# A product-key expert layer on one Trainium2 core: three of four token blocks go from gathered expert rows to a dense layer with a gate matrix

## The chip, the cores and the metric

One core of one Trainium2 chip runs the program. The metric is device time in microseconds of that core. The engines are TensorE (PE; its weight loads are listed as PEld), VectorE (DVE), ScalarE (ACT), GpSimd (POOL) and SyncE (SP), each with its own queue; they meet by semaphores. All data is float32.

## The reference

One decoder layer on x (1 x 512 x 1024):

```python
proj = x @ w_in                                   # 1024 -> 3584: seven groups of 512 columns
r = silu(rg) * GroupNorm(retention(rotary(rq), rotary(rk), rv))   # 4 heads of 128
d = 0.8 * RMSNorm((softmax(q1 k1^T) - lam * softmax(q2 k2^T)) v)  # 4 heads, causal
x = LayerNorm(alpha * x + concat(r, d) @ w_out)
q = (x @ w_query)                                 # 8 heads x 2 halves x 128
s = q . sub_keys                                  # 128 keys for each half
top_s, top_i = top_k(s, 16)                       # per half; then the best 16 of 256 sums
expert_idx = top_i[0] * 128 + top_i[1]            # 16384 experts
gate = softmax(best 16 sums)
ffn[t] = sum_e gate[t,e] * gelu(x[t] . u[expert_idx[t,e]]) * v[expert_idx[t,e]]   # 128 e per token
x = LayerNorm(alpha * x + ffn)
```

`peer_u` and `peer_v` are 16384 x 1024 each, 64 MB each. A token uses 128 of the 16384 rows of each.

## The kernel before

The 512 tokens are four blocks of 128. The work goes in two waves (`WAVES`, line 51): block 0 alone, then blocks 1 to 3. Each wave loads all 13 weight pieces of 2 MB (seven of `w_in`, two of `w_out`, four of `w_query`), so each is read twice.

**Mixer.** `fill_psum` (L509 and L515) runs the projections as eight accumulating matmuls per 512-wide bank. Rotary, decay, the norms, softmax's maxima and joins are on DVE; the exponentials and most copies out of PSUM are on ACT. `attend` (L661 scores, L681 transposes, L685 mix) goes head by head, then `mixed_out` transposes (L707) and multiplies by `w_out` (L716, L587 for block 0). `ln1` is LayerNorm 1. `query` (L744) makes the queries, 128 columns wide for block 0 and 384 for the second wave, and the key scores (L754).

**Retrieval.** `retrieve(b, s)` on DVE (L1269 to L1311) finds the 16 best keys and pairs of two heads of one block: `best_keys`, `best_pairs`, `best_experts`. A block has four such quarters, sixteen in all.

**Experts, block 0.** POOL gathers one row per token and expert slot (L438, 512 KB for 128 tokens, u rows and v rows separately) into a ring of 8. `dots` (L1039) multiplies a u row by the token and sums, on DVE. 32 v rows are added on PE through a diagonal matrix of gates (L461), 96 on DVE by `sums` (L1052). These groups of four, `rows(n)`, are interleaved by hand with the second wave's mixer work.

**Experts, blocks 1 to 3.** For each of 3 x 128 slots POOL gathers the u row and the v row of each token in one transfer of 1 MB (L426) into a ring of 18. DVE does the dot product (`pair_dot`, L1060), ACT the gelu of four slots (L971), DVE the weight (`weigh`, L1067), ACT writes the gates onto a diagonal (L979), PE adds v rows with two matmuls of 512 columns per slot (`add_pairs`, L474). The slot of the ring is free when PE has added it. The remaining ten quarters of the retrieval lie inside this loop on DVE. Last come `join_sums` and `finish` (LayerNorm 2) of each block.

## Time and profile before

| | |
|---|---|
| median of 3 runs | 1660.17 us (1654.67 to 1662.5) |
| span of the profiled execution, first to last instruction | 1633.5 us |
| PE busy | 1276.5 us (78%) |
| DVE busy | 1155.6 us (71%) |
| ACT busy | 267.2 us (16%) |
| POOL busy | 625.2 us (38%) |
| DMA moved | 603.44 MB, mean 369 GB/s |
| mean granted clock of PE | 0.896 |

The profiled execution's own time outside the profiler is not given apart from the three runs; its span lies 26.7 us under their median. Busy time is the union of an engine's instructions.
### The profile page before, as it was taken

What the parts mean: (1) busy time and instruction counts of PE and PEld (TensorE: products, weight loads), DVE (VectorE), ACT (ScalarE), POOL (GpSimd) and SP (SyncE); (2) the same over time, 40 slices, a digit from 0 to 9 for tenths busy, and PEclk for the clock granted to TensorE, in tenths of its full rate; (3) what the DMA queues carried; (4) which work ended last, traced back from release to release, by engine and by line L of the source; (5) the groups of instructions that cost most, each with busy time, mean ns of one, the idle gap of its engine ahead of it and who ended that gap; (6) DMA issues with size and microseconds to landing.
All of it is one profiled execution on the core that took longest, in us unless ns stands there. A gap on an engine that the chain in (4) does not pass through costs nothing.

```text
span 1633.5 us, 11511 instructions
## 1 busy us (share of the span) xinstructions
PE 1276.5 (78%) x3448; PEld 618.1 (38%) x3448; DVE 1155.6 (71%) x2727; ACT 267.2 (16%) x754; POOL 625.2 (38%) x645
## 2 busy tenths in 40 slices
PE   7879979888646994586978687878777878787885
PEld 5465446433323562232323233333333333332332
DVE  1349999767798979987676767776767677764454
ACT  0110000121211111121212121212121212121111
POOL 0004344474445565543434343434342434343320
PEclk9989999999767997798888888989897989899899
DMA  9939798897759898999999999999999999999993
GB/s 339 390 140 353 280 344 312 319 409 274 263 189 335 319 373 329 410 422 421 422 421 421 422 422 421 422 421 422 421 422 421 422 421 422 421 422 421 421 422 127
DMA packets 125710, 603.44 MB, mean 369 GB/s; under 512 B 12624, under 2 KB 14928, under 8 KB 76368
## 3 DMA queue, kind: packets, MB, share of 16 engines
q0 software_dynamic: 92160, 536.91, 81.2%
q1 hardware_dynamic: 33488, 65.80, 11.0%
q8 instruction: 27, 0.44, 0.1%
q14 instruction: 35, 0.29, 0.1%
HBM read 600.57 MB, written 2.10 MB: 369 GB/s over the span
## 4 chain that ended last, share of the span: by engine, by line
DMA 38%; PE 31%; DVE 23%; issue 3%; POOL 2%; SPq 1%; ACT 1%; DVEq 0%; POOLq 0%
DMA arena<-uv,idx 37%; PE W L474 7%; PE W L509 7%; DVE arena L1060 5%; PE ACC L474 4%; DVE xs L1052 4%; PE W L744 3%; PE W L716 3%; PE ACC L461 2%; POOL arena L438 2%; PE W L515 2%; DVE arena L1039 1%; DMA arena<-w_in 1%; DVE cand L1301 1%; DVE cand L1303 1%
## 5 line engine op out<-in xcount | busy, mean ns | idle before, releaser
L474 PE MATMUL W<-arena,fdiag 128*128 128x512 f32 x1024 | 498.9, 648 | 170.1 <-ACT fdiag L979 170.1
L426 POOL DMA_INDIRECT arena<-uv,idx x384 | 367.5, 957 | 586.7 <-PE W L474 355.7
L1060 DVE SCALAR_TENSOR_TENSOR arena<-arena,X 128x1024 f32<-128x1024 f32 x256 | 309.2, 1219 | 200.8 <-DMA arena<-uv,idx 199.7
L438 POOL DMA_INDIRECT arena<-uv,idx x256 | 257.3, 1005 | 372.2 <-DVE idx L1311 125.1
L474 PEld LDWEIGHTS W<-arena,fdiag 128*128 128x128 f32 x1024 | 208.6, 208 | 459.7 <-issue 253.0
L474 PE MATMUL ACC<-arena,fdiag 128*128 128x512 f32 x512 | 254.9, 660 | 69.3 <-ACT fdiag L979 69.3
L1060 DVE SCALAR_TENSOR_TENSOR arena<-arena,W 128x1024 f32<-128x1024 f32 x128 | 154.8, 1219 | 95.8 <-DMA arena<-uv,idx 95.4
L474 PEld LDWEIGHTS ACC<-arena,fdiag 128*128 128x128 f32 x512 | 107.0, 213 | 217.2 <-issue 132.1
L979 ACT ACTIVATE fdiag<-ident,gate 128x128 f32<-128x128 f32 x384 | 123.3, 390 | 354.7 <-DVE gate L1067 351.0
L1039 DVE SCALAR_TENSOR_TENSOR arena<-arena,X 128x1024 f32<-128x1024 f32 x128 | 150.0, 1216 | 24.8 <-DMA arena<-uv,idx 24.3
L509 PE MATMUL W<-arena 128*128 128x512 f32 x320 | 143.7, 605 | 9.7 <-DMA arena<-w_in 9.0
L1052 DVE SCALAR_TENSOR_TENSOR xs<-arena,gate,xs 128x1024 f32<-128x1024 f32 x96 | 123.3, 1284 | 19.3 <-DMA arena<-uv,idx 11.1
L744 PE MATMUL W<-arena 128*128 128x128 f32 (+1 forms) x512 | 116.8, 391 | 1.4 <-ACT arena L912 1.4
L971 ACT ACTIVATE hid<-hid 128x4 f32<-128x4 f32 x96 | 19.7, 205 | 456.5 <-DVE arena L1060 456.5
L744 PEld LDWEIGHTS W<-arena 128*128 128x128 f32 x512 | 80.2, 198 | 36.2 <-ACT arena L912 2.2
L509 PEld LDWEIGHTS W<-arena 128*128 128x128 f32 x320 | 60.8, 194 | 81.9 <-issue 76.9
L515 PE MATMUL W<-arena 128*128 128x128 f32 (+1 forms) x256 | 58.9, 388 | 10.8 <-DVE arena L1157 9.4
L461 PE MATMUL ACC<-arena,fdiag 128*128 128x512 f32 x128 | 59.0, 615 | 4.2 <-DMA arena<-uv,idx 4.2
L515 PEld LDWEIGHTS W<-arena 128*128 128x128 f32 x256 | 39.0, 194 | 28.4 <-issue 11.8
L716 PE MATMUL W<-arena 128*128 128x512 f32 x96 | 43.8, 616 | 0.7 <-ACT arena L912 0.7
L461 PEld LDWEIGHTS ACC<-arena,fdiag 128*128 128x128 f32 x128 | 24.5, 197 | 36.0 <-issue 29.7
L716 PEld LDWEIGHTS W<-arena 128*128 128x128 f32 x96 | 18.7, 198 | 25.1 <-issue 23.2
(178 smaller groups left out, 824.7 us busy)
## 6 DMA issues: line engine op xcount, KB each, us to landing
arena<-w_in SPq DMA_DIRECT2D x13, 2048.0 KB, 13.8
arena<-peer_w_query SPq DMA_DIRECT2D x8, 2048.0 KB, 14.4
arena<-uv,idx POOLq DMA_INDIRECT x640, 25.4
arena<-w_out SPq DMA_DIRECT2D x4, 2048.0 KB, 14.9
arena<-w_in SPq DMA_DIRECT2D x4, 512.0 KB, 6.4
out<-xs SPq DMA_DIRECT2D x4, 512.0 KB, 8.1
arena<-xT SPq DMA_DIRECT2D x1, 1536.0 KB, 18.2
xs<-x SPq DMA_DIRECT2D x1, 1536.0 KB, 17.0
```

The source lines that it names most:

```text
L426: pool.indirect_dma_start(out=fused[slot], out_offset=None, in_=uv, in_offset=bass.IndirectOffsetOnAxis(ap=idx[:, E + n:E + n + 1], axis=0 ...
L438: pool.indirect_dma_start(out=ring[:, r, :], out_offset=None, in_=rows, in_offset=bass.IndirectOffsetOnAxis(ap=idx[:, e:e + 1], axis=0), e ...
L461: last = nc.tensor.matmul(ACC[:, half * HW:(half + 1) * HW], fdiag[:, e % ND, :], ring[:, r, half * HW:(half + 1) * HW], start=e == 0, sto ...
L474: last = nc.tensor.matmul(sum_of(b)[:, half * HW:(half + 1) * HW], fdiag[:, n % ND, :], fused[n % NS][:, D + half * HW:D + (half + 1) * HW ...
L509: last = nc.tensor.matmul(bank, actT[:, k, part * P:(part + 1) * P], wts[slot][:, k, :], start=(k == 0), stop=(k == KD - 1))
L515: last = nc.tensor.matmul(bank[:, at:at + n_tok], wts[slot][:, k, h * P:(h + 1) * P], actT[:, k, toks], start=(k == 0), stop=(k == KD - 1))
L716: last = nc.tensor.matmul(W[:, 2 + half, :], mixT[:, k, :], wts[slot][:, k, :], start=(k == 0), stop=(k == KD - 1))
L744: last = nc.tensor.matmul(dst, wts[slot][:, k, i * P:(i + 1) * P], actT[:, k, toks], start=(k == 0), stop=(k == KD - 1))
L979: nc.scalar.activation(fdiag[:, n % ND, :], ident[:], ACT.Copy, scale=gate[:, E + n:E + n + 1]).then_inc(pair_diag_ready, 1)
L1039: STT(out=ring[:, r, :], in0=ring[:, r, :], scalar=1.0, in1=X[:], op0=ALU.mult, op1=ALU.mult, accum_out=hid[:, e:e + 1]).then_inc(slot_use ...
L1052: STT(out=xs[:, 0, :], in0=ring[:, r, :], scalar=gate[:, e:e + 1], in1=xs[:, 0, :], op0=ALU.mult, op1=ALU.add).then_inc(slot_used[r], 1)
L1060: STT(out=fused[slot][:, 0:D], in0=fused[slot][:, 0:D], scalar=1.0, in1=token_of(b), op0=ALU.mult, op1=ALU.mult, accum_out=hid[:, E + n:E ...
```

## The change

The mixer runs once for all four blocks: 28 projection banks in one go, then `attend` and `mixed_out` for blocks 0 to 3, and block 0's queries and key scores are placed beside blocks 1 and 2's attention (`beside`). Each weight piece of the mixer is read once, `w_query` twice. Block 0 still gathers its rows, 256 transfers of 512 KB into a ring of 6; DVE does all dots and all sums.

Blocks 1 to 3 gather nothing. Their expert layer is computed for all 16384 experts, in 128 tiles of 128 experts: `up` multiplies a tile of u (from a transposed copy `uT` that the host lays out) by 384 tokens, `hidden` applies gelu, `mask_hidden` multiplies by the gate matrix, which is zero for experts that the token did not pick, `add` multiplies by the tile of v for each of three blocks. The gate matrix is built token by token: DVE writes two one-hot matrices (`hot_quads`: picks x first key, and picks x second key), PE multiplies them (`quad`, four tokens at a time, each 128 x 128 columns), ACT copies the result to a staging tile and sends 2 MB of it per 32 tokens to a DRAM tensor `gd` of 25 MB (`take_quad`); it is read back by `load_g`, four tiles of experts at a time. 47 tiles of the hidden layer are held (`NH`): 23 are made before the gate matrix, 24 during it, and 81 in the last loop.

The order of the work is written out by hand in each engine's block. The core of the diff (lines that only rename or drop the old loops are left out):

```diff
+W_SLOTS = [0, 1, 2, 3, 0, 1, 2] + [0, 1] + [3, 2, 3, 2] + [0, 1, 0, 1]
+Q0, Q1 = WIN + WOUT, WIN + WOUT + WQ
+ROWS = 2 * E
+RING = 6
+ND = NB - 1
+TD = ND * P
+NT = P
+NH = 47
+UR = 4
+VR = 4
+LEAD = 6
+TAIL = 4
+QUADS = P // 4
+OH_RING = 4
+OH_BANKS = 5
+CHUNK = 32
+NC = TD // CHUNK
+PER_CHUNK = CHUNK // 4
+GT = 4
+UP_FIRST = NH - ND * QUADS // 4
...
+            def load_u(n):
+                if n >= UR:
+                    sp.wait_ge(u_ready, n - UR + 1)
+                elif n < 2:
+                    sp.wait_ge(diff_mixed, NB)
+                else:
+                    sp.wait_ge(mixer_ready, 2 * NB)
+                sp.dma_start(u_ring[n % UR], uT[n].rearrange("p (k e) -> p k e", k=KD)).then_inc(u_landed[n % UR], 16)
+            def load_v(n):
+                if n >= VR:
+                    sp.wait_ge(v_done, n - VR + 1)
+                sp.dma_start(v_ring[n % VR], uv[n * P:(n + 1) * P, D:2 * D]).then_inc(v_landed[n % VR], 16)
+            def load_g(g):
+                if g >= 2:
+                    sp.wait_ge(masked, GT * (g - 1))
+                src = gd[:, :, g * GT:(g + 1) * GT, :].rearrange("c j i t -> j c (i t)")
+                sp.dma_start(g_ring[g % 2], src).then_inc(g_landed[g % 2], 16)
...
+            for i in range(5, Q1 + 2):
+                load_w(i)
+            for n in range(UR):
+                load_u(n)
+            for i in range(Q1 + 2, Q1 + WQ):
+                load_w(i)
+            for n in range(UR, NH + UR):
+                load_u(n)
+            for i in range(2):
+                sp.wait_ge(spill_landed[i], 16 * (NC // 2))
+            load_g(0)
+            for n in range(VR):
+                load_v(n)
+            load_g(1)
+            sp.wait_ge(quad_ready, ND * QUADS)
+            for n in range(NT):
+                if n + VR < NT:
+                    load_v(n + VR)
+                if n + NH + UR < NT:
+                    load_u(n + NH + UR)
+                if n % GT == 1 and n // GT + 2 < NT // GT:
+                    load_g(n // GT + 2)
...
+            for s in range(ROWS):
+                e = s % E
+                if s < E and e % QUARTER == 0:
+                    pool.wait_ge(experts_ready, e // QUARTER + 1)
+                if s >= RING:
+                    pool.wait_ge(row_used[s % RING], s // RING)
...
+            def beside(b, h):
+                if (b, h) == (1, 1):
+                    turn_x1(0)
+                elif (b, h) == (1, 2):
+                    query_0(0)
+                elif (b, h) == (1, 3):
+                    query_0(1)
+                    key_scores_0(0)
+                elif (b, h) == (2, 0):
+                    query_0(2)
+                    key_scores_0(1)
+                elif (b, h) == (2, 1):
+                    query_0(3)
+                    key_scores_0(2)
+                elif (b, h) == (2, 2):
+                    key_scores_0(3)
+                elif (b, h) == (2, 3):
+                    turn_x1(1)
+                elif (b, h) == (3, 1):
+                    turn_x1(2)
...
+            def up(n):
+                pe.wait_ge(u_landed[n % UR], 16 * (n // UR + 1))
+                if n >= 2:
+                    pe.wait_ge(h_ready, n - 1)
+                for k in range(KD):
+                    last = nc.tensor.matmul(X[:, n % 2, 0:TD], u_ring[n % UR][:, k, :], actT[:, k, P:S],
+                                            start=(k == 0), stop=(k == KD - 1))
+                last.then_inc(u_ready, 1)
+            def turn_picks(d):
+                pe.wait_ge(pk_ready, d + 1)
+                if d:
+                    pe.wait_ge(pT_ready, d)
+                for c in range(3):
+                    last = nc.tensor.transpose(ACC[:, 1, c * P:(c + 1) * P], pk[d % 2][:, c, :], ident[:])
+                last.then_inc(pk_turned, 1)
+            def quad(q):
+                pe.wait_ge(hot_ready, q + 1)
+                if q >= OH_BANKS:
+                    pe.wait_ge(quad_taken, q - OH_BANKS + 1)
+                bank = quad_bank(q)
+                for m in range(4):
+                    last = nc.tensor.matmul(bank[:, m * P:(m + 1) * P], b_hot[:, q % OH_RING, m, :],
+                                            a_hot[:, q % OH_RING, m, :], start=True, stop=True)
+                last.then_inc(quad_ready, 1)
+            def add(n, d):
+                for half in range(2):
+                    last = nc.tensor.matmul(sum_banks(d)[:, half, :], h_slot(n)[:, d * P:(d + 1) * P],
+                                            v_ring[n % VR][:, half * HW:(half + 1) * HW],
+                                            start=(n == 0), stop=(n == NT - 1))
+                return last
...
+            project()
+            score(0, 0)
+            for b in range(NB):
+                attend(b)
+                mixed_out(b)
+            turn_x1(NB - 1)
+            query()
+            pe.wait_ge(scores_stored, 4 + ND * WQ)
+            for n in range(UP_FIRST):
+                up(n)
+            for d in range(ND):
+                turn_picks(d)
+                for q in range(d * QUADS, (d + 1) * QUADS):
+                    quad(q)
+                    if q % 4 == 3:
+                        up(UP_FIRST + q // 4)
+            pe.wait_ge(quad_taken, ND * QUADS)
+            for n in range(NT - TAIL):
+                pe.wait_ge(masked, n + 1)
+                pe.wait_ge(v_landed[n % VR], 16 * (n // VR + 1))
+                for d in range(ND):
+                    last = add(n, d)
+                last.then_inc(v_done, 1)
+                if n + NH < NT:
+                    up(n + NH)
+            pe.wait_ge(masked, NT)
+            for i in range(VR):
+                pe.wait_ge(v_landed[i], 16 * (NT // VR))
+            for d in range(ND):
+                for n in range(NT - TAIL, NT):
+                    last = add(n, d)
+                last.then_inc(acc_ready, 1)
...
+            def hidden(n):
+                act.wait_ge(u_ready, n + 1)
+                if n >= NH:
+                    act.wait_ge(v_done, n - NH + 1)
+                elif n >= 42:
+                    act.wait_ge(experts_ready, 16)
+                elif n >= 37:
+                    act.wait_ge(experts_ready, 12)
+                elif n >= 32:
+                    act.wait_ge(experts_ready, 8)
+                elif n >= 26:
+                    act.wait_ge(experts_ready, 4)
+                nc.scalar.activation(h_slot(n), X[:, n % 2, 0:TD], ACT.Gelu).then_inc(h_ready, 1)
+            def take_picks(d):
+                act.wait_ge(experts_ready, 4 * d + 8)
+                nc.scalar.activation(pk[d % 2][:, 2, :], pk[d % 2][:, 2, :], ACT.Exp).then_inc(pk_exp_ready, 1)
+                act.wait_ge(pk_turned, d + 1)
+                if d == 2:
+                    act.wait_ge(hot_ready, QUADS)
+                nc.scalar.activation(pT[d % 2], ACC[:, 1, 0:3 * P].rearrange("p (c t) -> p c t", c=3),
+                                     ACT.Copy).then_inc(pT_ready, 1)
+            def take_quad(q):
+                c, at = divmod(q, PER_CHUNK)
+                act.wait_ge(quad_ready, q + 1)
+                if at == 0 and c >= 2:
+                    act.wait_ge(spill_landed[c % 2], 16 * (c // 2))
+                nc.scalar.activation(stage[c % 2][:, :, 4 * at:4 * at + 4],
+                                     quad_bank(q).rearrange("p (m i) -> p i m", m=4), ACT.Copy).then_inc(quad_taken, 1)
+                if at == PER_CHUNK - 1:
+                    act.wait_ge(quad_taken, q + 1)
+                    nc.scalar.dma_start(gd[c], stage[c % 2]).then_inc(spill_landed[c % 2], 16)
...
+            project()
+            for b in range(NB):
+                attention(b)
+                take_mixed(b)
+            take_x1(NB - 1)
+            query()
+            act.wait_ge(experts_ready, 4)
+            nc.scalar.activation(gate[:], gate[:], ACT.Exp).then_inc(gate_exp_ready, 1)
+            for n in range(UP_FIRST):
+                hidden(n)
+            for d in range(ND):
+                take_picks(d)
+                for q in range(d * QUADS, (d + 1) * QUADS):
+                    take_quad(q)
+                    if q % 4 == 3:
+                        hidden(UP_FIRST + q // 4)
+            for n in range(NH, NT):
+                hidden(n)
+                if n == NH + 60:
+                    for i in range(RING):
+                        last_dot = max(s for s in range(E) if s % RING == i)
+                        act.wait_ge(row_used[i], last_dot // RING + 1)
+                    nc.scalar.activation(hid[:], hid[:], ACT.Gelu).then_inc(gelu_ready, 1)
...
+            def dot(s):
+                r = s % RING
+                dve.wait_ge(row_landed[r], row_landings(s))
+                STT(out=ring[r], in0=ring[r], scalar=1.0, in1=xs[:, 0, :], op0=ALU.mult, op1=ALU.mult,
+                    accum_out=hid[:, s:s + 1]).then_inc(row_used[r], 1)
+            def weigh():
+                gate_norm(gate[:], gate_exp_ready, 1)
+                residual(0)
+                dve.wait_ge(gelu_ready, 1)
+                link(TT(out=gate[:], in0=gate[:], in1=hid[:], op=ALU.mult))
+            def add_row(s):
+                r = s % RING
+                dve.wait_ge(row_landed[r], row_landings(s))
+                if s > E:
+                    dve.wait_ge(row_used[(s - 1) % RING], (s - 1) // RING + 1)
+                STT(out=xs[:, 0, :], in0=ring[r], scalar=gate[:, s - E:s - E + 1], in1=xs[:, 0, :],
+                    op0=ALU.mult, op1=ALU.add).then_inc(row_used[r], 1)
...
+            def norm_picks(d):
+                dve.wait_ge(pk_exp_ready, d + 1)
+                g = pk[d % 2][:, 2, :].rearrange("p (h k) -> p h k", h=PH)
+                link(nc.vector.reduce_sum(gsum[:], g, AX.X))
+                link(nc.vector.reciprocal(gsum[:], gsum[:]))
+                TT(out=g, in0=g, in1=gsum[:].unsqueeze(2).to_broadcast([P, PH, TOPK]),
+                   op=ALU.mult).then_inc(pk_ready, 1)
+            def hot_quads(d):
+                dve.wait_ge(pT_ready, d + 1)
+                for q in range(d * QUADS, (d + 1) * QUADS):
+                    if q >= OH_RING:
+                        dve.wait_ge(quad_ready, q - OH_RING + 1)
+                    for m in range(4):
+                        t = 4 * (q % QUADS) + m
+                        TS(b_hot[:, q % OH_RING, m, :], iota_f[:], pT[d % 2][:, 1, t:t + 1], None, ALU.is_equal)
+                        last = TS(a_hot[:, q % OH_RING, m, :], iota_f[:], pT[d % 2][:, 0, t:t + 1],
+                                  pT[d % 2][:, 2, t:t + 1], ALU.is_equal, ALU.mult)
+                    last.then_inc(hot_ready, 1)
+            def mask_hidden(n):
+                g = n // GT
+                if n % GT == 0:
+                    dve.wait_ge(g_landed[g % 2], 16 * (g // 2 + 1))
+                dve.wait_ge(h_ready, n + 1)
+                h = h_slot(n).rearrange("p (c t) -> p c t", c=NC)
+                TT(out=h, in0=h, in1=g_ring[g % 2][:, :, n % GT * CHUNK:(n % GT + 1) * CHUNK],
+                   op=ALU.mult).then_inc(masked, 1)
...
+                    if (b, h) in ((2, 1), (3, 1)):
+                        best_keys(0, b - 2)
+                    elif (b, h) in ((2, 2), (3, 2)):
+                        best_pairs()
+                    elif (b, h) in ((2, 3), (3, 3)):
+                        best_experts(0, b - 2)
...
+            best_keys(0, 2)
+            best_pairs()
...
+            best_experts(0, 2)
+            retrieve(0, 3)
+            rows(8)
+            for s in range(4):
+                retrieve(1, s)
+            best_keys(2, 0)
+            norm_picks(0)
+            best_pairs()
+            best_experts(2, 0)
+            hot_quads(0)
+            for s in range(1, 4):
+                retrieve(2, s)
+            best_keys(3, 0)
+            norm_picks(1)
+            best_pairs()
+            best_experts(3, 0)
+            hot_quads(1)
+            for s in range(1, 4):
+                retrieve(3, s)
+            norm_picks(2)
+            rows(4)
+            hot_quads(2)
+            for n in range(LEAD):
+                mask_hidden(n)
+            for n in range(NT):
+                if n + LEAD < NT:
+                    mask_hidden(n + LEAD)
+                if n == 62:
+                    weigh()
+                rows(min(2, E - taken[0]) if n < 62 else 2)
+                if n == NT - 1:
+                    rows(ROWS - taken[0])
+                    finish(0)
+            for d in range(ND):
+                join_sums(d)
+                finish(d + 1)
```

## Rows read from the trace of the kernel before

**Rows 1.** Stretches: PE, PEld, DVE, ACT, POOL busy; PEclk, DMA share, GB/s

```profile
150.00:200.00 50.00, 50.00 (x136) 23.44 (x135) 48.76 (x133) 4.67 (x8) 18.20 (x20) 1.00 0.82 314
...
450.00:500.00 50.00, 21.02 (x73) 12.20 (x72) 45.78 (x83) 9.44 (x26) 22.47 (x19) 0.60 0.61 208
...
800.00:1000.00 200.00, 158.49 (x320) 66.96 (x320) 134.37 (x344) 39.27 (x111) 74.93 (x80) 0.88 1.01 421
```

**Rows 2.** Chain that ended last, shares, from the page

```profile
DMA 38%; PE 31%; DVE 23%; issue 3%; POOL 2%; SPq 1%; ACT 1%; DVEq 0%; POOLq 0%
DMA arena<-uv,idx 37%; PE W L474 7%; PE W L509 7%; DVE arena L1060 5%; PE ACC L474 4%; DVE xs L1052 4%; PE W L744 3%; PE W L716 3%; PE ACC L461 2%; POOL arena L438 2%; PE W L515 2%; DVE arena L1039 1%; DMA arena<-w_in 1%; DVE cand L1301 1%; DVE cand L1303 1%
```

**Rows 3.** Who waited for whom

```profile
ACT fdiag L979 <- DVE gate L1067: 351.0, 95, 7.4
DVE arena L1060 <- DMA arena<-uv,idx: 295.2, 246, 2.2
```

**Rows 4.** Groups by line and form: us busy, mean ns

```profile
L474 PE MATMUL W<-arena,fdiag 128*128 128x512 f32 x1024 | 498.9, 648 | 170.1 <-ACT fdiag L979 170.1
...
L1060 DVE SCALAR_TENSOR_TENSOR arena<-arena,X 128x1024 f32<-128x1024 f32 x256 | 309.2, 1219 | 200.8 <-DMA arena<-uv,idx 199.7
...
L474 PE MATMUL ACC<-arena,fdiag 128*128 128x512 f32 x512 | 254.9, 660 | 69.3 <-ACT fdiag L979 69.3
...
L1052 DVE SCALAR_TENSOR_TENSOR xs<-arena,gate,xs 128x1024 f32<-128x1024 f32 x96 | 123.3, 1284 | 19.3 <-DMA arena<-uv,idx 11.1
```

**Rows 5.** Pieces of the chain in order of time: start, length

```profile
108.46 7.16 PE W L744 x64
...
187.09 20.62 PE W L509 x48
...
259.25 5.16 PE W L515 x16
```

**Rows 6.** PE in order of time: first projection, attention, output, queries

```profile
6.03 8.62 PE L509 MATMUL W<-arena 128*128 128x512 f32 x16 [6.03 <-DMA arena<-w_in]
...
428.09 1.65 PE L685 MATMUL W<-arena 128*128 128x128 f32 x6 [0.58 <-ACT arena L888]
434.93 1.97 PE L707 MATMUL W<-ident,arena 128*128 128x128 f32 x8 [5.19 <-DVE arena L1243]
...
439.89 14.00 PE L716 MATMUL W<-arena 128*128 128x512 f32 x32
...
466.82 2.08 PE L661 MATMUL W<-dkT,arena 64*128 64x512 f32 x4 [9.06 <-ACT arena L880]
...
476.34 2.08 PE L661 MATMUL W<-dkT,arena 64*128 64x512 f32 x4
...
503.73 15.82 PE L716 MATMUL W<-arena 128*128 128x512 f32 x32 [0.69 <-ACT arena L912]
...
530.04 23.22 PE L744 MATMUL W<-arena 128*128 128x384 f32 x64 [0.69 <-ACT arena L912]
...
626.52 3.00 PE L754 MATMUL W<-arena 128*128 128x128 f32 x24 [0.58 <-ACT arena L929]
...
1615.56 7.13 PE L474 MATMUL W<-arena,fdiag 128*128 128x512 f32 x16 [0.62 <-ACT fdiag L979]
```

**Rows 7.** DVE in order of time: first and last of a retrieval quarter

```profile
555.67 0.87 DVE L1269 MAX8 best_v<-rv 128x8 f32<-128x128 f32 x4 [0.76 <-ACT rv L935]
...
571.26 0.19 DVE L1311 SCALAR_TENSOR_TENSOR idx<-sel 128x32 int32<-128x32 f32 x1
```

**Rows 8.** DVE groups by form, small scalar operations

```profile
L1189 DVE TENSOR_SCALAR arena<-W,mv,rstd 128x128 f32<-128x128 f32 x16 | 5.5, 404 | 0.1
...
L1214 DVE TENSOR_SCALAR arena<-arena,rz 128x256 f32<-128x256 f32 x4 | 1.5, 372 | 0.1
```

**Rows 9.** DMA issues by source: count, KB each, median us to landing

```profile
arena<-w_in SPq DMA_DIRECT2D x13, 2048.0 KB, 13.8
...
arena<-xT SPq DMA_DIRECT2D x1, 512.0 KB, 3.8
```

More of the change, by code:

```diff
@@ L806, in take_fill @@
                     act.wait_ge(proj_ready, n + 1)
[L807 to L814 removed]
+                    act.wait_ge(rot_ready, rots(n))
@@ L873, in attention, with project @@
-            def attention(b, beside):
+                    dst = {RV: rv, DV: dv, DQ: dqT, DKK: dkT}[g][:, part, :]
+                    nc.scalar.activation(dst, bank, ACT.Copy).then_inc(proj_taken_act, 1)
+                if n and FILLS[n - 1][0] in (RQ, RK):
+                    take_rotated(rots(n) - 1)
+            def project():
+                for n in range(len(FILLS)):
+                    take_fill(n)
+                    if n == fills_of(RV)[0]:
+                        act.wait_ge(lam_dots_ready, 1)
+                        nc.scalar.activation(lam[:, 2:4], lam[:, 0:2], ACT.Exp).then_inc(lam_exp_ready, 1)
@@ L874, in attention @@
+            def attention(b):
                 keys_n = (b + 1) * P
@@ new lines, in store_scores, with query @@
+            def store_scores(b, s, bank):
+                act.wait_ge(keys_scored, 4 + ND * s + b if b else s + 1)
+                nc.scalar.activation(scores[b][:, s * HW:(s + 1) * HW], bank, ACT.Copy).then_inc(scores_stored, 1)
+            def query():
+                for n in range(4, 20):
+                    s, i = divmod(n - 4, 4)
+                    act.wait_ge(query_ready, n + 1)
+                    if s and i == 0:
+                        act.wait_ge(keys_scored, 4 + s * ND)
+                    nc.scalar.activation(qq[:, i, :], W[:, 2 + n % 2, 0:TD], ACT.Copy).then_inc(query_taken, 1)
+                    if i == 3:
+                        for j in range(ND):
+                            store_scores(1 + j, s, W[:, (s * ND + j) % 2, :])
```

998 lines of the change are left out of this document (304 added, 694 removed).

## The prediction

> **What bounds the kernel now.** I read the chain first, then the waits, then the stretches. The chain [rows 2] gives 37% of the span to the gathers of experts (uv by idx) and 31% to PE in many small shares: no engine's own work sets most of the end, the transfers do. The stretches [rows 1] show where. From 650 us on, memory moves 421 or 422 GB/s without a pause: 384 slots of 1 MB, about 403 MB, in some 970 us. PE is busy for only 158.48 of 200 us there, with a granted clock of 0.88, and both waits [rows 3] agree: DVE waited 295.2 us for gathered rows, and ACT waited 351.0 us for the weights that DVE makes from them. Before 650 us it is another kernel: PE has stretches with no gap at all (50.00 of 50 us at clock 1.00) and stretches with long ones (21.02 of 50 at 0.60), where attention goes head by head.
>
> So the question is whether 403 MB of gathers at 422 GB/s cost more than what stands in for them. The new work is PE's, so I need PE's price at full clock. A projection bank, eight matmuls of 512 columns, takes 20.62 / 3 = 6.87 us [rows 5], so 0.859 us per matmul; eight of 384 columns take 5.16 us, 0.645 each; 32 of 128 columns take 7.16 us, 0.224 each. `up` has the same form as the 384-column row, `add` and `fill_psum` that of the 512-column one.
>
> **PE's work alone.** up: 128 tiles x 5.16 = 660 us. add: 128 x 6 x 0.859 = 660 us. The gate matrix: 384 x 0.224 = 86 us. Projections: 28 x 6.87 = 192 us. Output: 4 x 14.0 = 56 us [rows 6]. Queries: 4 x 7.16 + 16 x 5.16 = 111 us. Key scores, retention and transposes: some 50 us. Sum about 1815 us, without a single wait, against a span of 1633.5 us. What goes: 768 add matmuls of the same form, which took 498.9 + 254.9 = 754 us of busy time at the lower clock [rows 4] and were hidden by the gathers. What the change saves in DMA (some 360 MB left of 603: 134 for both tables, 134 of gathers, 50 for the gate matrix, the rest weights) was the bound, but PE's sum is already longer than the whole kernel.
>
> **The new order, stage by stage.**
>
> Projections. PE starts at 6.0 us [rows 6]; 28 banks are 192.4 us; four transposes for each of 8 rotated banks cost 0.5 us (half of 1.97 us for eight, which ran at half clock), so 4; retention's 80 matmuls of 128 columns are 18 us. The rest of xT is in the queue ahead of the second bank, a few us: 4. End at 224 us. The weights don't hold it: a 2 MB piece lands in 13.8 us [rows 9] and lasts 27.5.
>
> Attention and output, four blocks. A head of block 3 took 476.34 - 466.82 = 9.5 us with four gathered rows on DVE in it [rows 6]; they cost 4 x 1.28 [rows 4], which leaves 4.4 us. Sixteen heads: 70. From the last mix of a block (429.7) to its output matmuls (439.9) are 10.2 us of squares, norm, transposes and copies: 41. Output 56. LN1 delays the second head of three blocks by about 5: 15. What stands `beside`: 4 x 7.16 + 4 x 1.9 + 3 x 2.0 = 42 on PE, of which each of 11 pieces hides about 1 behind the join: 31. DVE's six thirds of two retrieval quarters (15.8 us each, 555.67 to 571.45 [rows 7]) are 32, a third of it beside PE's pieces: 21. The first head of three blocks runs under the output matmuls: -12. Sum 222, and 10.5 from the last output matmul to the first query (519.55 to 530.04): 456 us.
>
> Queries. The code of the second wave is unchanged, 530.04 to 629.52 is 99.5 us: 556 us. Block 1's retrieval on DVE, four quarters of 15.8, keeps pace and ends by 575.
>
> First 23 ups: 119 us, to 675. Here the change adds a wait: `take_picks(0)` stands behind `hidden(22)` in ACT's queue, so the exponentials that `norm_picks(0)` needs come only now, and DVE, queued behind that wait with block 2's and 3's retrieval, idles for some 95 us. Then best_pairs and best_experts (two thirds of 15.8) and the transposes: 12, to 687.
>
> Gate matrix. Four quads and an up are 16 x 0.224 + 5.16 = 8.7 us of PE; a block is 8 of these, with waits 73 us. DVE has to write 32 one-hot tiles in the same time. No row has this form. Above stands the 128-column operation with two scalars from PSUM, 5.5 / 16 = 0.344 us [rows 8]; below, the four 128-wide operations in 0.87 us, 0.22 each [rows 7]; a 256-column one with one scalar from SBUF, 0.372, lies outside but shows that the second scalar and PSUM are what makes 0.344. I take 0.25, so 8.0 us: hidden by 8.7, barely. At 0.344 it is 11.0 and DVE sets the pace. Three blocks: 219. Between blocks PE has nothing: three quarters of retrieval, best_keys, then pairs and experts, 64 us less the 7 that DVE is ahead, so 57; and before the third, three quarters, the exponentials and four rows, 54 - 7 = 47. That gives 687 + 219 + 104 = 1010.
>
> Spill and read back. The last 2 MB go out (13.8 us as a load [rows 9], my only price) and 768 KB in runs of 512 bytes come back (3.8 us for 512 KB in such runs, so 5.8): 20. At 422 GB/s both would take 7, at 13.8 each 28; these are the bounds. To 1030.
>
> Last loop. 768 adds are 660, 81 ups 418: 1078 us, to 2108. What lies under it: DVE per tile one 384-wide product (about 0.55, from 1219 ns for 1024 columns [rows 4]) and two rows (2.6) against 10.3 and later 5.15; the DMA moves 2.3 MB in 10.3 us, later 1.8 MB in 5.15, 344 GB/s against 422 shown. `load_g` waits for `masked` and holds the loads of u and v queued on SP behind it, but DVE is six tiles ahead. Cost taken: 0. At the 314 GB/s of the stretch from 150 us [rows 1] the last 47 tiles would take 0.5 us more each, 23 us; if each of their 12 gate loads stalls PE for its own landing, 60; that is the upper bound. No gain below 0, since PE's matmuls are all there.
>
> End. From PE's last four matmul pairs (1622.7) to the span's end, 10.8 us [rows 6]: 2119. The profiled span lies 26.7 us under the median of the runs, so the time is 2119 + 27 = 2146 us.
>
> **A rule against the rows.** The rows give 0.859 us for a 512-column float32 matmul in an unbroken stream, as three banks back to back in 20.62 us show [rows 5]. The Trainium skill, TensorE: Matmul & The Clock Gate, section Back-to-back issue gap, gives a sustained spacing of about 131 ns for 512 columns in a stream of weight loads and matmuls, and 216 ns for an isolated one; its page FP8 and Floating Point Precision counts four passes for true float32. Four of the first are an estimate of 524 ns, four of the second 864 ns. The trace sides with the second. By the first the sum would be about 515 us shorter, 1631 us.
>
> **Rivals.**
> *The stream gets cheaper* (the other side: faster). Place: `up` and `add`. If a stream a thousand us long overlaps its passes better than one of 50 us, the 1320 us of the two shrink; the point is 486 us, that is 0.54 us per 512 columns in place of 0.859. At 0.53 the kernel takes 1640 us. Against it: stretches of 20.62 us and 50.00 of 50 us busy show no trend. The Trainium skill's 131 ns, above, is this rival. Chance 0.03, a third of it within half a per cent of no change.
> *DVE sets the pace of the gate matrix.* 0.344 per one-hot tile: 88 us per block in place of 73, and the 7 us ahead are lost: +60, 2206 us. For it: only 0.7 us lie between the two engines. Chance 0.19.
> *The clock.* If small waits in the last loop keep the granted clock at 0.88, as in the gathering stage [rows 1], 1078 becomes 1225: 2293 us. Against it: it was 1.00 wherever PE had no gap. Chance 0.09.
> *The front is shorter.* If the pieces beside attention hide in its gaps (52 us) and the retrieval overlaps somewhat better: -60, 2086 us. Chance 0.19.
> My forecast, 2146 us with its own range of 2110 to 2190, has 0.50.
>
> **How the numbers follow.** Half a per cent of 1660 us is 8 us, about what a measurement of this kernel can tell from no change. Every case but the first lies over 400 us above it, so slower gets 0.97, faster 0.02, the same 0.01. The range takes in the shorter front (2086, and 26 below for the spill and the ends of the heads), the gate matrix at DVE's pace and nearly all of the clock's case: 2060 to 2290.
>
> **What would show it.** In the new profile: PE busy near 1800 us and over 85%; 128-tile loop of about 10.3 us per tile down to 5.15, with clock 1.00; DVE idle about 95 us before the first picks are normed and PE idle twice for about 50 us in the gate stage; one-hot operations near 0.25 us; DMA around 360 MB. Wrong: `up` at under 5 us per tile, or a last loop that starts before 900 us.

## The result

The changed kernel takes 2126.62 us, median of 4 runs (2124.38 to 2129.2), against 1658.34 us for the kernel before, run beside it: a ratio of 1.282, 95% interval 1.279 to 1.284. The forecast was 2146, between 2060 and 2290.

The page of the profiled execution (span 2125.4 us, time 2127.21): the busy share of PE, the transfers, the chain that ended last, the costliest groups (busy, mean ns, idle before), and two DMA sources (count, KB, us to landing).

```profile
PE 1892.4 (89%) x6017; PEld 1042.1 (49%) x6017; DVE 957.2 (45%) x2767; ACT 207.8 (10%) x433; POOL 332.5 (16%) x261
...
DMA packets 149312, 366.78 MB, mean 173 GB/s; under 512 B 11120, under 2 KB 62576, under 8 KB 147568
...
PE 83%; DVE 12%; DMA 2%; ACT 1%; issue 1%; POOL 0%; SPq 0%; DVEq 0%
PE X L663 30%; PE W L690 19%; PE ACC L690 10%; PE W L460 6%; PE W L644 4%; PE W L591 3%; PE W L683 3%; PE W L457 3%; PE ACC L619 1%; DMA arena<-gd 1%; PE ACC L683 1%; DVE lng L1193 1%; DVE cand L1161 1%; DVE cand L1159 1%; PE W L653 1%
...
L663 PE MATMUL X<-arena 128*128 128x384 f32 x2048 | 678.0, 486 | 0.7 <-ACT dkT L838 0.7
...
L690 PE MATMUL W<-arena 128*128 128x512 f32 x768 | 349.6, 598 | 16.7 <-DMA arena<-uv 16.7
L1204 DVE TENSOR_TENSOR arena<-arena 128x384 f32<-128x384 f32 x96 | 52.6, 555 | 487.2 <-DMA arena<-gd 487.2
...
L690 PE MATMUL ACC<-arena 128*128 128x512 f32 x384 | 180.3, 592 | 0.0
...
L1193 DVE TENSOR_SCALAR lng<-iota_f,both_uses 128x128 f32<-128x128 f32 x384 | 137.2, 357 | 0.0
...
L1192 DVE TENSOR_SCALAR arena<-iota_f,both_uses 128x128 f32<-128x128 f32 x384 | 114.0, 297 | 21.5 <-PE W L683 16.8
...
L683 PE MATMUL W<-lng,arena 128*128 128x128 f32 x616 | 81.3, 290 | 23.3 <-DVE lng L1193 23.3
...
gd<-arena ACTq DMA_DIRECT2D x12, 2048.0 KB, 6.5
arena<-gd SPq DMA_DIRECT2D x32, 768.0 KB, 6.1
```

The chain has turned over [rows 2]: 83% PE where the gathers had 38%. PE is busy for 1892.4 us, more than the whole kernel before. `up` (L663) is 678.0 us, and `add` (L690) 349.6 + 180.3 = 529.9 in the records shown (1152 of its 1536 records are in these groups; the rest lie in groups by other home tiles of the hidden layer). The records of `up` are its 1024 matmuls, two for each. PE's busy time is 77 us over the 1815 us of my sum, which counted every matmul at full clock; the stretch of attention below ran at 0.76. What else makes up the 77 us was not taken apart. The bytes fell from 603.44 to 366.78 MB, and the time did not follow them.

The stretches, with the columns of [rows 1]:

```profile
224.00:456.00 232.00, 155.16 (x659) 96.86 (x660) 124.54 (x426) 41.97 (x135) 5.79 (x6) 0.76 0.18 62
456.00:557.00 101.00, 98.00 (x355) 61.08 (x354) 74.38 (x271) 15.28 (x29) 10.59 (x8) 0.97 0.27 99
557.00:677.00 120.00, 119.31 (x374) 70.31 (x373) 19.40 (x90) 13.25 (x26) 0.00 (x0) 1.00 0.31 97
677.00:778.00 101.00, 73.95 (x388) 56.03 (x387) 89.74 (x381) 28.19 (x46) 0.00 (x0) 0.88 0.35 131
778.00:822.00 44.00, 1.92 (x8) 1.52 (x8) 42.14 (x164) 0.80 (x2) 0.00 (x0) 0.50 0.00 0
...
1062.00:1500.00 438.00, 438.00 (x1191) 226.10 (x1190) 112.28 (x202) 21.12 (x43) 109.15 (x83) 1.00 0.65 222
...
1895.00:2110.00 215.00, 207.76 (x481) 91.45 (x479) 133.91 (x158) 0.00 (x0) 95.40 (x74) 0.98 0.84 306
```

In the last loop PE is busy 438.00 of 438 us at clock 1.00 and the DMA moves 222 GB/s; in the gathering stage [rows 1] PE had 79% at 0.88 and the DMA 421. The stretch of 778 to 822 is the opposite, PE 1.92 of 44 us while DVE works 42.14.

PE in order of time (start, length; in brackets the idle time before and who ended it). First three pieces round the first ups, then the gaps between the blocks of the gate matrix with the start of the last loop, then PE's last matmuls:

```profile
558.35 118.95 PE L663 MATMUL X<-arena 128*128 128x384 f32 x368 [0.69 <-ACT dkT L838]
680.45 0.55 PE L673 MATMUL ACC<-ident,both_uses 128*128 128x128 f32 x3 [3.15 <-DVE both_uses L1181]
692.53 6.81 PE L683 MATMUL W<-lng,arena 128*128 128x128 f32 x32 [11.53 <-DVE lng L1193]
```

```profile
808.90 0.90 PE L673 MATMUL ACC<-ident,both_uses 128*128 128x128 f32 x3 [43.26 <-DVE both_uses L1181]
820.98 3.89 PE L683 MATMUL W<-lng,arena 128*128 128x128 f32 x16 [11.18 <-DVE lng L1193]
...
932.37 0.90 PE L673 MATMUL ACC<-ident,both_uses 128*128 128x128 f32 x3 [38.51 <-DVE both_uses L1181]
938.77 2.08 PE L683 MATMUL ACC<-lng,arena 128*128 128x128 f32 x8 [5.50 <-DVE lng L1193]
...
1006.36 5.33 PE L663 MATMUL X<-arena 128*128 128x384 f32 x16
1021.18 6.13 PE L690 MATMUL W<-arena 128*128 128x512 f32 x8 [9.50 <-DMA arena<-uv]
```

```profile
2106.62 3.60 PE L690 MATMUL ACC<-arena,rv 128*128 128x512 f32 x8
```

The first 23 ups run 118.95 us without a break. Between the first and the second block's quads PE waits 43.26 + 11.18 us, between the second and third 38.51 + 5.50, and before the last loop 9.50. Waits of other engines, and PE's own by line (us, times, longest):

```profile
POOL arena L421 <- DVE arena L939: 1033.6, 17, 442.6
...
DVE arena L1204 <- DMA arena<-gd: 487.2, 24, 39.2
...
DVE gsum L1179 <- ACT both_uses L870: 102.8, 2, 102.4
```

```profile
PE ACC L673 <- DVE both_uses L1181: 84.9, 3, 43.3
PE W L683 <- DVE lng L1193: 23.3, 3, 11.5
...
PE W L690 <- DMA arena<-uv: 16.7, 2, 9.5
```

DVE's 102.4 us on `gsum` are the wait for the exponentials, which stand behind the first 23 `hidden` in ACT's queue. DVE waits 487.2 us more for the gate matrix in the last loop, which costs nothing, since it is ahead of PE there; PE itself waits for data 16.7 us in all.

### The profile page after: what moved, and what is told of

It reads as the page before. It is cut to its first block, busy times and chain, and to the rows that moved or that the text cites. A ratio compares the mean times of both kernels' runs of the same rounds, so it can differ in the third digit from the quotient of the medians.

```text
span 2125.4 us, 16625 instructions
## 1 busy us (share of the span) xinstructions
PE 1892.4 (89%) x6017; PEld 1042.1 (49%) x6017; DVE 957.2 (45%) x2767; ACT 207.8 (10%) x433; POOL 332.5 (16%) x261
## 2 busy tenths in 40 slices
DMA packets 149312, 366.78 MB, mean 173 GB/s; under 512 B 11120, under 2 KB 62576, under 8 KB 147568
## 4 chain that ended last, share of the span: by engine, by line
PE 83%; DVE 12%; DMA 2%; ACT 1%; issue 1%; POOL 0%; SPq 0%; DVEq 0%
PE X L663 30%; PE W L690 19%; PE ACC L690 10%; PE W L460 6%; PE W L644 4%; PE W L591 3%; PE W L683 3%; PE W L457 3%; PE ACC L619 1%; DMA arena<-gd 1%; PE ACC L683 1%; DVE lng L1193 1%; DVE cand L1161 1%; DVE cand L1159 1%; PE W L653 1%
## 5 line engine op out<-in xcount | busy, mean ns | idle before, releaser
L663 PE MATMUL X<-arena 128*128 128x384 f32 x2048 | 678.0, 486 | 0.7 <-ACT dkT L838 0.7
L421 POOL DMA_INDIRECT arena<-uv,idx x256 | 332.1, 1297 | 1752.0 <-DVE arena L939 1033.6
L663 PEld LDWEIGHTS X<-arena 128*128 128x128 f32 x2048 | 387.2, 190 | 282.9 <-issue 38.7
L690 PE MATMUL W<-arena 128*128 128x512 f32 x768 | 349.6, 598 | 16.7 <-DMA arena<-uv 16.7
L1204 DVE TENSOR_TENSOR arena<-arena 128x384 f32<-128x384 f32 x96 | 52.6, 555 | 487.2 <-DMA arena<-gd 487.2
L690 PEld LDWEIGHTS W<-arena 128*128 128x128 f32 x768 | 147.3, 192 | 190.0 <-issue 173.3
L690 PE MATMUL ACC<-arena 128*128 128x512 f32 x384 | 180.3, 592 | 0.0
L939 DVE SCALAR_TENSOR_TENSOR arena<-arena,xs 128x1024 f32<-128x1024 f32 x128 | 152.2, 1222 | 6.0 <-DMA arena<-uv,idx 5.6
L460 PE MATMUL W<-arena 128*128 128x512 f32 x320 | 142.9, 603 | 6.6 <-DMA arena<-w_in 6.3
L1193 DVE TENSOR_SCALAR lng<-iota_f,both_uses 128x128 f32<-128x128 f32 x384 | 137.2, 357 | 0.0
L1192 DVE TENSOR_SCALAR arena<-iota_f,both_uses 128x128 f32<-128x128 f32 x384 | 114.0, 297 | 21.5 <-PE W L683 16.8
L690 PEld LDWEIGHTS ACC<-arena 128*128 128x128 f32 x384 | 73.0, 190 | 91.8 <-issue 91.8
L683 PE MATMUL W<-lng,arena 128*128 128x128 f32 x616 | 81.3, 290 | 23.3 <-DVE lng L1193 23.3
L644 PE MATMUL W<-arena 128*128 128x384 f32 x256 | 85.7, 497 | 0.7 <-ACT arena L823 0.7
L591 PE MATMUL W<-arena 128*128 128x512 f32 x128 | 63.8, 662 | 0.7 <-ACT arena L815 0.7
L457 PE MATMUL W<-arena 128*128 128x512 f32 x128 | 56.1, 592 | 0.0
```

The lines of the kernel that those rows point to most:

```text
L421: pool.indirect_dma_start(out=ring[s % RING], out_offset=None, in_=rows, in_offset=bass.IndirectOffsetOnAxis(ap=idx[:, e:e + 1], axis=0), ...
L457: last = nc.tensor.matmul(bank, wts[slot][:, k, part * P:(part + 1) * P], actT[:, k, :], start=(k == 0), stop=(k == KD - 1))
L460: last = nc.tensor.matmul(bank, actT[:, k, part * P:(part + 1) * P], wts[slot][:, k, :], start=(k == 0), stop=(k == KD - 1))
L591: last = nc.tensor.matmul(W[:, 2 + half, :], mixT[:, k, :], wts[slot][:, k, :], start=(k == 0), stop=(k == KD - 1))
L644: last = nc.tensor.matmul(W[:, 2 + n % 2, 0:TD], wts[slot][:, k, i * P:(i + 1) * P], actT[:, k, P:S], start=(k == 0), stop=(k == KD - 1))
L663: last = nc.tensor.matmul(X[:, n % 2, 0:TD], u_ring[n % UR][:, k, :], actT[:, k, P:S], start=(k == 0), stop=(k == KD - 1))
```

## Experiments

The kernel before was run beside each group of runs, and the groups ran on different chips. Its time was 1658.34 us (median) beside the changed kernel, 1636.36 (median) beside e1 to e4, 1654.87 (median) beside e5 to e7, and 1648.39 (one run) beside e8 and e9. The times of e1, e5 and e6 are medians of four runs, those of e2, e3, e4, e7, e8 and e9 single runs. Savings are counted from the 2126.62 us of the changed kernel.

### The same work in a better order (e1)

```diff
 # ACT
+            for n in range(UP_FIRST):
+                hidden(n)
+                if n in (5, 18):
+                    exp_picks(n // 18)
 # PE and ACT: ups after which quad
-                    if q % 4 == 3:
-                        up(UP_FIRST + q // 4)
+UPS_AFTER = {4 * i + 3: (UP_FIRST + i,) for i in range(8)}
+UPS_AFTER[2 * QUADS - 1] = tuple(range(UP_FIRST + 8, UP_FIRST + 19))
+UPS_AFTER.update({2 * QUADS + 4 * i + 3: (UP_FIRST + 19 + i,) for i in range(5)})
+                    for n in UPS_AFTER.get(q, ()):
+                        up(n)
...
 # DVE, the new order
+            norm_picks(0)
+            for s in range(4):
+                retrieve(2, s)
+            norm_picks(1)
+            best_keys(3, 0)
+            best_pairs()
+            hot_quads(0)
+            hot_quads(1)
+            best_experts(3, 0)
+            for s in range(1, 4):
+                retrieve(3, s)
```

> Same work as the changed kernel, another order. ACT makes the exponentials of block 1's picks after hidden(5) and of block 2's after hidden(18) instead of behind hidden(22); DVE runs block 2's whole retrieval while PE does the first 23 ups; eleven of the ups that stood between quads stand together where DVE retrieves block 3. Theory (PE's own work sets the end, and the waits for DVE between the blocks of the gate matrix are added to it): the first quads start about 11 us earlier, PE's idle time of 43 + 11 us before the second block goes nearly away, of the 38 + 5 before the third too, and the quads without ups go at DVE's pace of about 7.2 us per four; last loop begins near 940 us in place of 1021, time 2050, ratio to before 1.235. Rival (the last loop is bound by something else that follows the clock on the wall, such as the row gathers of block 0): the loop grows by what the gate stage gives, time within 20 us of 2127.

Measured: 2062.29 us, ratio 1.260 (1.256 to 1.263), 64 us less than the changed kernel. PE in order of time, only pieces after a wait:

```profile
681.45 1.16 PE L686 MATMUL W<-lng,arena 128*128 128x128 f32 x8 [2.64 <-DVE lng L1203]
...
758.44 1.16 PE L686 MATMUL W<-lng,arena 128*128 128x128 f32 x8 [2.57 <-DVE lng L1203]
...
875.52 0.55 PE L676 MATMUL ACC<-ident,both_uses 128*128 128x128 f32 x3 [3.08 <-DVE both_uses L1191]
881.92 2.08 PE L686 MATMUL ACC<-lng,arena 128*128 128x128 f32 x8 [5.85 <-DVE lng L1203]
...
959.27 5.27 PE L693 MATMUL W<-arena 128*128 128x512 f32 x8 [13.95 <-DMA arena<-uv]
```

The quads start at 681.45 as expected, the second block's after 2.57 us of waiting, the third's after 3.08 + 5.85. The last loop starts at 959.27, 61.9 us earlier, and from there to the end of the span are 1102.3 us against 1104.2 in the changed kernel. So nearly all of the gain is idle time of PE, and none was given back. It was 12 us less than expected: quads without ups go at 1.81 us each, 57 us for a block, as forecast, but the third block, with five ups in it, took 63 us, and the wait for the gate matrix's way through DRAM grew to 13.95 us, for here no up follows the last quads and covers a part of it.

### Half of the adds, in both kernels (e2, e3)

```diff
 # add (changed kernel) and add_pairs (kernel before)
-                for half in range(2):
+                for half in range(1):
```

> The changed kernel; add makes only the first 512 of the 1024 output columns, so half of the v product of blocks 1 to 3 is left out. All transfers, all of DVE's and ACT's work stay. Theory (PE bound): 384 matmuls of 0.859 us go, 330 us, until the transfers or DVE take over; a tile costs 7.7 us in the first 81 and in the last 47, at 2.6 us of PE, the DMA's 1.8 MB at 400 to 422 GB/s set 4.3 to 4.5 us. So -209 - 35 = about -245 us: 1880. Rival (transfers set the last loop already): under 60 us less.

> The kernel before with the same edit: add_pairs makes only the first 512 of the 1024 output columns, half of the v product of blocks 1 to 3 is left out. All gathers stay. Theory (the gathers set the end, PE's 754 us are hidden): within 8 us of the kernel before, 1658. Rival (PE shares the bound): 50 us less or more.

Measured: 1888.71 us for the dense kernel, 238 less. The gathering kernel took 1633.58, where seven runs without the edit took 1633.61 to 1640.78: nothing that can be told from no change. Stretches of the dense one, then of the gathering one:

```profile
1021.00:1500.00 479.00, 479.00 (x1360) 258.61 (x1359) 165.59 (x296) 30.15 (x62) 156.78 (x116) 1.00 0.82 291
...
1648.00:1852.00 204.00, 137.58 (x284) 57.34 (x282) 127.99 (x127) 0.49 (x1) 98.16 (x82) 0.83 0.99 363
```

```profile
800.00:1000.00 200.00, 99.23 (x160) 38.74 (x159) 133.40 (x342) 38.84 (x110) 74.00 (x80) 0.75 1.01 421
```

One edit takes 384 matmuls out of either kernel, 330 us at full clock. In the gathering kernel PE falls from 158.49 to 99.23 busy us of 200 [rows 1], and even its granted clock falls, from 0.88 to 0.75; the transfers stay at 421 GB/s, as does the time. In the dense kernel PE stays at 479.00 of 479 and simply gets through sooner, until the last 47 tiles. They take 204 us, 4.3 each as expected; there PE is busy for 137.58 us, the DMA's share is 0.99, and the transfers have taken over. That is the bound changing hands, seen from both sides.

### Half of each up (e8)

```diff
-                for k in range(KD):
+                for k in range(KD // 2):
```

> The changed kernel; up contracts over only 512 of the 1024 features, four matmuls in place of eight, so half of each hidden value's sum is left out. Transfers stay. Theory (PE's sum sets the end wherever it is not waiting for DVE): the first 23 ups lose 59 us; the gate stage goes at DVE's 7.2 us in place of 8.7 per four quads, 24 groups, 35 us, but its gaps grow by the 7 us that DVE was ahead, twice, so 21; the 81 ups of the last loop lose 209. Together -289: 1838. Rival (the last loop falls to its transfers at 2.3 MB per 7.7 us, 300 GB/s): 60 us or more above that.

Measured: 1833.99 us, 293 less, where 289 were expected. In the last loop PE has no gap with 290 GB/s under it:

```profile
1000.00:1500.00 500.00, 500.00 (x1295) 245.69 (x1294) 176.18 (x292) 31.62 (x65) 162.41 (x125) 1.00 0.83 290
```

### Without block 0's rows (e4)

```diff
-            for s in range(ROWS):
+            for s in range(12):
                 e = s % E
...
 # DVE, last loop
-                rows(min(2, E - taken[0]) if n < 62 else 2)
```

> The changed kernel with block 0's experts left out except for the first 12 row gathers: 244 of 256 gathers, their dots and sums on DVE are gone. Theory (hidden under PE in the last loop): no change up to 8 us less, 2120 to 2127; what may go is a wait for v of some us at the loop's end. Rival (the gathers press on the transfers of u, v and the gate matrix or on DVE in the last 47 tiles): 20 to 60 us less.

The lines not shown let the wait for the rows, the gelu and the gates go over 12 columns, and drop the last `rows`. Measured: 2122.28 us, 4.3 less in a single run, and 2.1 under the fastest run of the changed kernel. The loop's stretch has half the traffic and the same PE:

```profile
1062.00:1500.00 438.00, 438.00 (x1191) 226.03 (x1190) 19.65 (x40) 21.07 (x43) 0.00 (x0) 1.00 0.37 120
```

244 gathers, 128 MB and 294 us of DVE's busy time (957.2 to 663.4) were hidden, but for these 4 us, of which 2.5 are PE's waits for tiles of v (16.7 to 14.2). The forecast's last loop took them as zero.

### The dense layer with cheap matmuls (e5, e6)

```diff
...
+        ub = part(16 * K, D).bitcast(BF).rearrange("p (i k e) -> p i k e", i=2, k=KD)
+        vb = part(16 * K + D, D).bitcast(BF).rearrange("p (i d) -> p i d", i=2)
+        xb = actT[:, :, 0:TD // 2].bitcast(BF)
 # ACT, one tile ahead of hidden(n)
+                    nc.scalar.activation(ub[:, n % 2], u_ring[n % UR], ACT.Copy).then_inc(u_cast, 1)
+                nc.scalar.activation(vb[:, n % 2], v_ring[n % VR], ACT.Copy).then_inc(v_cast, 1)
 # PE
-                    last = nc.tensor.matmul(X[:, n % 2, 0:TD], u_ring[n % UR][:, k, :], actT[:, k, P:S],
+                    last = nc.tensor.matmul(X[:, n % 2, 0:TD], ub[:, n % 2, k, :], xb[:, k, :],
 # DVE writes the masked hidden layer in bfloat16
-                TT(out=h, in0=h, in1=g_ring[g % 2]
+                TT(out=h_low(n).rearrange("p (c t) -> p c t", c=NC), in0=h, in1=g_ring[g % 2]
```

Not shown: the row ring's four slots in place of six, the new semaphores, the loads of u and v, which now wait for the cast and not for the matmul, and the last four tiles, whose adds go tile by tile in place of block by block.

> The changed kernel with up and add in bfloat16: ACT rounds each tile of u and v and the 384 tokens to bfloat16, the masked hidden layer is written in bfloat16, so the experts of blocks 1 to 3 are computed in lower precision; the row ring has 4 slots in place of 6 to make room. Bytes moved are the same. Theory (what made the dense layer slow is PE's price of 0.859 us for a float32 matmul of 512 columns): up and add fall to about a quarter, 1.3 us for each group of eight or six; the first 23 ups take about 42 us at ACT's pace, the gate stage goes at DVE's pace of 7.2 us per four quads, and the last loop is set by its transfers, 2.3 MB per tile at 422 GB/s or 5.5 us, later 4.3: 650 us in place of 1089. Time 1580, faster than the gathers. Rival (the mixed transfers, with 512-byte runs, don't pass 250 GB/s, or ACT's casts set the pace): last loop 850 us or more, time over 1780.

> The same in the order of e1: exponentials of the picks early, block 2's retrieval under the first ups, eleven ups together. Theory: DVE alone paces the gate stage now, and its idle time before the picks of block 1, some 25 us with the short ups, goes: 25 to 35 us less than e5, about 1550. Rival (the order gained by PE's idle time only, so with PE cheap it gives nothing): within 8 us of e5.

Measured: e5 1632.13 us, ratio 0.987 (0.984 to 0.990); e6, with e1's order, 1617.58 us, ratio 0.977 (0.974 to 0.980), beside 1654.87 for the kernel before. So 494 us of the changed kernel's 2126 went with the cheaper matmuls, although the same edit gives ACT two casts per tile and leaves the rows a smaller ring, and 15 more went with the order. These two kernels do lower-precision work against a kernel that stays in float32; the gathering kernel with bfloat16 tables was not tried. The last loop of e6 in its two parts, the 81 tiles with an up and the 47 without, then two waits of the second part:

```profile
901.00:1349.00 448.00, 262.75 (x1134) 113.35 (x1134) 220.76 (x349) 198.85 (x244) 164.12 (x147) 0.85 1.04 393
1349.00:1569.00 220.00, 102.33 (x282) 30.38 (x282) 131.69 (x132) 49.03 (x48) 98.88 (x87) 0.68 0.97 353
```

```profile
PE W L706 <- DVE arena L1254: 85.2, 32, 6.7
DVE xs L1005 <- DMA arena<-uv,idx: 81.0, 63, 4.3
```

In the first part the DMA's share is full, 393 GB/s, PE is busy for 262.75 of 448 us, and a tile takes 448 / 81 = 5.5 us, as expected. In the second 47 tiles were expected at 4.3 us, 202 us, and took 220 at 353 GB/s. There DVE waits for rows (81.0 us), its masking stands in the queue behind them, and PE waits for that (85.2 us). When PE has made its last add, at 1569 us, DVE still adds rows of block 0, to 1586, and then normalises four blocks one after another: 50 us to the end of the span, where the changed kernel needs 15.2. In e5 the two parts and the end are 443, 223.5 and 48 us, so of the 52 us by which it was over its expectation 17 are in the loop, expected at 650, and 33 behind it. Whether the ring of four rows did it was not tried by itself. e2, with six slots and no casts, moved the same last 47 tiles in 204 us and then took 35 to the end, which speaks for the ring or the casts, but doesn't part them. The order gave 15 us where 25 to 35 were expected. Three PE pieces of one tile:

```profile
1114.56 1.02 PE L706 MATMUL W<-arena,kT 128*128 128x512 bf16 x4 [1.01 <-ACT arena L883]
...
1115.42 0.59 PE L706 MATMUL ACC<-arena,kT 128*128 128x512 bf16 x2
...
1117.03 1.47 PE L679 MATMUL X<-arena 128*128 128x384 bf16 x8 [1.02 <-ACT arena L876]
```

The first four matmuls of 512 columns start at 1114.56 and the next at 1115.42, so they are 0.215 us apart, a quarter of float32's 0.859. Eight of 384 columns are listed with 1.47 us, the tail of the last one included, where float32's are listed with 5.33.

### The same without the rows (e9)

The edit of e4 on the kernel of e6.

> The kernel of e6 (bfloat16 up and add, the better order) with block 0's experts left out except for the first 12 row gathers. Theory (with PE's price gone the transfers set the last loop, 392 GB/s in e6): a tile moves 1.25 MB in place of 2.3, the loop goes at 3.2 to 3.6 us per tile and later at 1.8 to 2.7 in place of 5.9 and 4.8, so 300 us less than e6, 1320. The same edit took 5 us off the changed kernel, whose loop PE sets. Rival (the chain cast, up, gelu, mask sets e6's loop): under 100 us less.

Measured: 1284.36 us, 333 less than e6, where the same edit took 4 us off the changed kernel. The stretch lies in the tiles with an up:

```profile
900.00:1100.00 200.00, 173.29 (x868) 85.43 (x868) 30.54 (x63) 147.38 (x184) 0.00 (x0) 0.95 1.06 384
```

The transfers still run at 384 GB/s, with ACT's casts and PE close behind (147.38 and 173.29 of 200 us). A tile with an up takes 3.2 us, as expected, in place of e6's 5.5 (the expectation had e6's tiles at 5.9 and 4.8; its trace has 5.5 and 4.7). At nearly the same rate a tile moves 1.25 MB in place of 2.3, so there it is the bytes that cost. In the last 47 tiles and behind them the edit takes away transfers and DVE's work on rows together, and what each of the two costs was not separated. So the rows, which cost next to nothing under float32 matmuls, are worth a fifth of the kernel with cheap ones.

### The changed kernel again (e7)

> The changed kernel once more, on the chip of this call, where the kernel before may take 1636 us as in the last call or 1658 as in the first. Theory (before is set by the gathers' rate, which differs from chip to chip, the changed kernel by PE): 2127 within 4 us whichever the kernel before takes. Rival (the chips differ in everything alike): 2100 where the kernel before takes 1636.

Measured: 2128.03 us beside 1654.87. The kernel before was near its first value here, so this run doesn't tell the two theories apart. What speaks for the first is e1, beside which the kernel before took 1636.36: from the start of the last loop to the end of the span are 1102.3 us in e1, 1104.2 in the changed kernel and 1106.0 in this run. PE's loop is the same to 0.3% where the gathering kernel differs by 1.3%. A run of the changed kernel itself beside 1636 us was not made, and why the gathering kernel differs was not shown.

## Why the prediction was right

By its own steps, forecast and then measured:

| step | forecast | measured |
|---|---|---|
| first query on PE | 456 | 458.1 |
| queries | 99.5 | 100.2 (to 558.35) |
| first 23 ups | 119 | 118.95 |
| to the first quad | 12 | 15.2 (692.53) |
| four quads and an up | 8.7 | 8.73 |
| PE idle between blocks | 57 and 47 | 54.4 and 44.0 |
| three blocks of quads and ups | 219 | 220.7 |
| end of the last quads' up | 1010 | 1011.7 |
| gate matrix through DRAM | 20 | 9.5 |
| last loop | 1078 | 1089.0 (1021.18 to 2110.22) |
| from there to the span's end | 10.8 | 15.2 |
| span | 2119 | 2125.4 |
| outside the span | 27 | 1.8 |
| time | 2146 | 2126.62 |

**Which step failed.** The last one. I put 26.7 us outside the span because the profiled execution's span lay that far under the median of the runs. Here time less span is 2127.21 - 2125.4 = 1.8 us, and it is the same 1.8 in the runs of the kernel before that stand beside e1 (1636.36 and 1634.5). So the kernel before's profiled execution took about 1635 us itself, like the 1636.36 beside e1: what I read as a fixed cost was a faster execution. That the gathers were faster in it is argued, not shown, for no trace of a slower execution was kept. It is the one term whose origin I couldn't name in a row, and it explains 25 us, where the forecast was 19 over and its span 6 under.

That the span is only 6 us off is luck in part: it has the gate matrix 10.5 us too long and the last loop 11 us too short.

**The gate matrix through DRAM** was mis-sized. I had priced a 2 MB store by a 2 MB load in a crowded queue, 13.8 us [rows 9]; it lands in 6.5, and the read back in 6.1 against my 5.8. And the last store was sent at 1007.19 us, while the last up still ran to 1011.69, an overlap of 4.5 us that my sum left out.

**The last loop** is 11 us longer. After the wait of 9.50 us the first adds began at half clock, 6.13 us for what is listed with 3.60 later. PE waited once for a tile of v, 7.24 us, at 2080: the adds of the last four tiles wait for all four slots of v's ring, and the last load can only be sent when the tile before them has been added. My sum had no term for this wait. The adds behind it were slow once more, 5.37 for 3.60. The stall of `load_g` didn't occur: its waits for `masked` sum to 0.6 us.

**The end** is 4.4 us longer: the sums of blocks 1 to 3 come within 14 us of each other, and DVE normalises all four blocks one after another at 7.6 us each; the kernel before had only its last block left there.

**The rivals.** *The stream gets cheaper* is dead: over 833 us without a gap (1062 to 1895), clock 1.00, ups and adds take 5.16 and 5.15 us as in 20 us of the kernel before. The Trainium skill's 131 ns for 512 columns (TensorE: Matmul & The Clock Gate, Back-to-back issue gap) would make four passes 524 ns, by estimate; this float32 stream stays at 859 ns, four times 215, and e6's bfloat16 matmuls start 215 ns apart. So here the measurement decides against the page. The four passes for true float32 of the Trainium skill (FP8 and Floating Point Precision, TensorE Precision Notes) agree with the experiment that removed them: 0.215 us in e6 beside 0.859. *DVE sets the pace of the gate matrix* did not come: a pair of one-hot tiles takes 0.45 us, 0.225 each, below my 0.25; the group's 8.73 us are PE's. With the ups taken out (e1) DVE does set it, 1.81 us per quad. *The clock* did not stay down in the last loop: 1.00 from 1062 us on, and 0.98 in its last stretch. *The front is shorter* did not come: attention and output took what the sum of heads, tails and pieces gave, 224 to 458, at a granted clock of 0.76. Here too two errors cancel: the four blocks' output matmuls took 15.9 us each in place of 14.0, 8 us in all, and the way from a block's last mix to them 7.4 to 9.4 us in place of 10.2, 7 us less in all.

That PE's price is the cause is shown by e2, e3, e5 and e8 together: half the adds cost 238 us here and nothing there, half of each up is worth 293, and with both at a quarter the dense layer takes 1.3% less time than the gathers, and 2.3% less in the better order. That DVE's waits add to it is shown by e1. The gain of reading the mixer's weights once was not tested by itself; the queries of blocks 1 to 3 end at 558 us in place of 630, but the kernel before has done all of block 0's rows by 664, and the changed one has used only eight of their 256 when its first ups begin.

## What to carry to other kernels

Before trading transfers for arithmetic, add up the arithmetic alone at its measured price and set it beside the whole kernel: 1815 us of matmuls against a span of 1633.5 decided this case before any schedule was drawn, and saving 40% of the bytes changed nothing once PE had no gap. Whether a dense layer pays in place of gathered rows hung here on the price of one matmul, 0.859 us in float32 and 0.215 in bfloat16, and even then the gain was small. And what is free under one bound is dear under the next: the same rows cost 4 us and 333 us.

## What was not expected of the hardware

The same gathering kernel took 1636.36 to 1658.34 us in four groups of runs, 1.3% apart, with the runs of one group within 0.6%, while the PE-bound loop was the same to 0.3%. The mixed transfers of e6, a third of the kernel's packets being between 512 bytes and 2 KB long, kept 393 GB/s, closer to the gathers' 421 than to the 314 that I had held against them. In the changed kernel a one-hot tile of 128 columns with one scalar takes up 0.20 us of DVE and one with two scalars 0.25 us, from its start to the next one's, though they are listed with 297 and 357 ns.
